# A two-block transformer kernel on one core: the normalising passes of five layer norms on VectorE instead of GpSimd, and half of a depthwise convolution as diagonal matmuls on TensorE

## What is computed

```python
h = layer_norm(ALPHA * h + 0.5 * swiglu_ffn(h, w13, w2), g0, b0)
h = layer_norm(ALPHA * h + token_mix(h, ...), g1, b1)
h = layer_norm(ALPHA * h + 0.5 * swiglu_ffn(h, w13, w2), g2, b2)
```

```python
u = a * sigmoid(gate)                 # a, gate: 256 columns each of h @ w_in
y = depthwise_conv(u, w_dw) + b_dw    # 31 taps, each channel for itself, left-padded
y = silu(layer_norm(y)) @ w_pw
```

## Time and profile before

| what | us |
|---|---|
| median of 3 runs | 1914.4 (1910.63 to 1915.46) |
| the profiled execution, its own time | 1913.0 |
| its span, first to last instruction | 1911.2 |
| TensorE busy | 1737.0 (91%) |
| VectorE busy | 1191.8 (62%) |
| ScalarE busy | 837.8 (44%) |
| GpSimd busy | 435.3 (23%) |
| mean granted TensorE clock | 0.956 of full speed |

### The profile page before, as it was taken

One profiled execution on the slowest core, in us unless ns is written; L12 is line 12 of the kernel. 1 busy time (PEld: TensorE's weight loads), 2 busy tenths in 40 slices (PEclk: granted clock), 3 DMA queues, 4 the chain that ended last, 5 costly groups with the idle time before them and its releaser, 6 DMA issues.

```text
span 1911.2 us, 32538 instructions
## 1 busy us (share of the span) xinstructions
PE 1737.0 (91%) x13186; PEld 1664.5 (87%) x13186; DVE 1191.8 (62%) x1561; ACT 837.8 (44%) x1116; POOL 435.3 (23%) x380
## 2 busy tenths in 40 slices
PE   7999968899999999968889996998999977779998
PEld 6999966699999999966689995987899976579997
DVE  5555588785556655587785544566656456466654
ACT  5334464353335333464353333663443346544333
POOL 0003576340045002576240042220000001300000
PEclk9999988999999999989999997997999989789999
DMA  6555433145543555423145542343355423025552
GB/s 214 172 174 201 150 103 105 66 144 180 179 181 131 176 176 191 156 103 110 67 167 176 192 182 88 114 141 111 111 182 209 172 96 116 17 103 192 180 204 82
DMA packets 37233, 277.67 MB, mean 145 GB/s; under 512 B 4304, under 2 KB 4432, under 8 KB 7072
## 3 DMA queue, kind: packets, MB, share of 16 engines
q1 hardware_dynamic: 36016, 271.73, 40.5%
q0 software_dynamic: 1136, 4.83, 0.7%
HBM read 275.49 MB, written 1.05 MB: 145 GB/s over the span
## 4 chain that ended last, share of the span: by engine, by line
PE 75%; DVE 12%; ACT 6%; POOL 3%; issue 3%; DMA 0%; SPq 0%; DVEq 0%; ACTq 0%; POOLq 0%
PE bank L635 23%; PE bank L637 23%; PE bank L636 23%; DVE w_lo L1679 3%; ACT w_hi L1156 2%; POOL y L566 2%; PE bank L653 1%; DVE conv_y L1958 1%; DVE rstd L1687 1%; DVE o_rstd L2047 1%; ACT h L1206 1%; ACT h_hi L1205 1%; POOL h L545 1%; ACT att_p L1482 0%; DVE qk_raw L1967 0%
## 5 line engine op out<-in xcount | busy, mean ns | idle before, releaser
L1679 DVE TENSOR_TENSOR w_lo<-raw,w_hi 128x2048 fp32r<-128x2048 f32 (+2 forms) x241 | 598.5, 2484 | 256.5 <-ACT w_hi L1156 256.0
L635 PE MATMUL bank<-h_hi,w_hi 128*128 128x272 f32 (+1 forms) x2336 | 676.3, 289 | 47.7 <-DVE w_lo L1679 27.0
L637 PE MATMUL bank<-h_hi,w_lo 128*128 128x272 f32 (+1 forms) x2336 | 674.2, 289 | 0.0
L636 PE MATMUL bank<-h_lo,w_hi 128*128 128x272 f32 (+1 forms) x2336 | 673.9, 288 | 0.0
L1156 ACT ACTIVATE w_hi<-raw 128x2048 fp32r<-128x2048 f32 (+2 forms) x241 | 486.1, 2017 | 144.6 <-PE bank L637 144.1
L635 PEld LDWEIGHTS bank<-h_hi,w_hi 128*128 128x128 f32 x2336 | 447.4, 192 | 52.0 <-DVE w_lo L1679 32.1
L637 PEld LDWEIGHTS bank<-h_hi,w_lo 128*128 128x128 f32 x2336 | 447.1, 191 | 0.0
L636 PEld LDWEIGHTS bank<-h_lo,w_hi 128*128 128x128 f32 x2336 | 446.5, 191 | 0.0
L635 PE MATMUL bank<-g_hi,w_hi 128*128 128x272 f32 (+1 forms) x1344 | 392.2, 292 | 12.5 <-DVE y L1705 4.9
L637 PE MATMUL bank<-g_hi,w_lo 128*128 128x272 f32 (+1 forms) x1344 | 386.2, 287 | 0.0
L636 PE MATMUL bank<-g_lo,w_hi 128*128 128x272 f32 (+1 forms) x1344 | 385.7, 287 | 0.0
(11 more groups left out here) (296 smaller groups left out, 1982.2 us busy)
## 6 DMA issues: line engine op xcount, KB each, us to landing
raw<-in_up_w SPq DMA_DIRECT2D x131, 1024.0 KB, 4.9
raw<-in_down_w SPq DMA_DIRECT2D x48, 1408.0 KB, 5.9
raw<-in_in_w SPq DMA_DIRECT2D x20, 1024.0 KB, 4.9
raw<-in_out_w SPq DMA_DIRECT2D x16, 1024.0 KB, 4.9
raw<-in_even_w SPq DMA_DIRECT2D x12, 1024.0 KB, 4.9
...
decay<-in_decay POOLq DMA_DIRECT2D x1, 1632.0 KB, 8.1
```

Source lines behind the costliest of these rows:

```text
L635: pe.matmul(out, w[0], x[0], start=first, stop=False)
L636: pe.matmul(out, w[0], x[1], start=False, stop=False)
L637: return pe.matmul(out, w[1], x[0], start=False, stop=last)
L1679: dve.tensor_tensor(w_lo[:, slot, 0:blocks * P], raw[:, slot, 0:blocks * P], w_hi[:, slot, 0:blocks * P].bitcast(F32), ALU.subtract).then_ ...
```

## The change

It has three parts.

1. The eight normalising passes of each norm are issued by VectorE (`renormalise`, in the order below) and no longer by GpSimd. The parts of VectorE's program around them are written in another order, and so are ScalarE's: the six later tiles stand in one row between the splits of chunks 3 and 4. A feed-forward block now defers three chunks, not four; chunk 3 goes to banks 6 and 7.
2. The 31 taps of channels 128 to 255 are matmuls: weights are 128x128 matrices with a tap's 128 coefficients on the diagonal, the moving operand is `upad` shifted by the tap, in plain float32, summed in bank 5. 16 taps stand in TensorE's program behind chunk 5 of the input product, 15 behind chunk 7. GpSimd's queue loads the matrices, 1 MB in front of each part, the second when the first is used. ScalarE copies the sum out with the bias, in chunk 9. The old product and addition loop on GpSimd is gone.
3. VectorE's half of the convolution adds even taps into `conv_y` and odd ones into `acc`, each waiting for the tap before the last, with one addition at the end.

The core of the diff. GpSimd:

```diff
-            def normalise():
...
-                for p in pairs:
-                    pool.tensor_tensor(p, p, both_tiles(mu), ALU.subtract).then_inc(t1_ready, 1)
-                pool.wait_ge(rstd_ready, seen.next(rstd_ready))
-                for p in pairs:
-                    pool.wait_ge(t1_ready, seen.next(t1_ready))
-                    pool.tensor_tensor(p, p, both_tiles(rstd), ALU.mult).then_inc(t_ready, 1)
...
                 pool.wait_ge(conv_in, seen.next(conv_in))
-
-                def product(i):
-                    if i >= 3:
-                        pool.wait_ge(conv_sum, seen.at(conv_sum, i - 1))
-                    pool.tensor_scalar(conv_t[:, i % 2, :], upad[:, 1, i:i + T], taps[:, i:i + 1], 0.0,
-                                       ALU.mult, ALU.add).then_inc(conv_mul, 1)
-
-                pool.tensor_scalar(conv_y[:, 1, :], upad[:, 1, 0:T], taps[:, 0:1], taps[:, TAPS:TAPS + 1],
-                                   ALU.mult, ALU.add).then_inc(conv_sum, 1)
-                product(1)
-                for i in range(1, TAPS):
-                    if i + 1 < TAPS:
-                        product(i + 1)
-                    pool.wait_ge(conv_mul, seen.at(conv_mul, i))
-                    pool.wait_ge(conv_sum, seen.at(conv_sum, i))
-                    pool.tensor_tensor(conv_y[:, 1, :], conv_y[:, 1, :], conv_t[:, i % 2, :], ALU.add)\
-                        .then_inc(conv_done if i == TAPS - 1 else conv_sum, 1)
-                seen.skip(conv_mul, TAPS - 1)
-                seen.skip(conv_sum, TAPS - 1)
+                pool.dma_start(diag[:], a["conv_w"][l, 0]).then_inc(diag_loaded, 16)
+                pool.wait_ge(diag_used, l + 1)
+                pool.dma_start(diag[:], a["conv_w"][l, 1]).then_inc(diag_loaded, 16)
                 residual_sums(2)
```

TensorE:

```diff
+                def conv_taps(c):
+                    for part in range(2):
+                        if c != CONV_AT[part]:
+                            continue
+                        pe.wait_ge(conv_in, l + 1)
+                        pe.wait_ge(diag_loaded, (2 * l + part + 1) * 16)
+                        for i in range(part * TAP_HALF, min((part + 1) * TAP_HALF, TAPS)):
+                            last = pe.matmul(ps[5][:, 0:T], diag[:, i % TAP_HALF, :], upad[:, 1, i:i + T],
+                                             start=i == 0, stop=i == TAPS - 1)
+                        last.then_inc(conv_mm if part else diag_used, 1)
+                in_tiles(IN_GROUPS, IN_ORDER, VALUES, [m for _, m in KTOK], 4, z_copied, T, conv_taps, DEFER)
```

ScalarE:

```diff
+            def renormalise(l, i):
+                split_next(UP_BLOCKS, 0, 2)
+                for k in range(2):
+                    normed_tile(l, i, k)
+                split_next(UP_BLOCKS, 0, 3)
+                for k in range(2, KD):
+                    normed_tile(l, i, k)
+                split_next(UP_BLOCKS, 0, 4)
...
+                            renormalise(*norm)
+                            deferred_silu(0)
+                            deferred_silu(1)
+                            split_next(UP_BLOCKS, 0, 5)
+                            deferred_silu(2)
...
+                def conv_copy(c):
+                    if c == 9:
+                        act.wait_ge(conv_mm, l + 1)
+                        act.activation(conv_y[:, 1, :], ps[5][:, 0:T], ACT.Identity, bias=vcol(l, V_CDB + 1))\
+                            .then_inc(conv_done, 1)
```

VectorE:

```diff
+            def renormalise(take):
+                pairs = [y[:, 2 * j:2 * j + 2, :] for j in range(KD // 2)]
+                def less_mean(j):
+                    dve.tensor_tensor(pairs[j], pairs[j], both_tiles(mu), ALU.subtract).then_inc(t1_ready, 1)
+                def by_deviation(j):
+                    dve.wait_ge(t1_ready, seen.next(t1_ready))
+                    dve.tensor_tensor(pairs[j], pairs[j], both_tiles(rstd), ALU.mult).then_inc(t_ready, 1)
 
                 dve.wait_ge(mean_ready, seen.next(mean_ready))
                 dve.tensor_scalar(mu[:], ps[6][:, 0:T], 1.0 / D, None, ALU.mult).then_inc(mu_ready, 1)
-                split_next(early, 0, 1)
+                split_next(UP_BLOCKS, 0, 1)
                 dve.wait_ge(var_ready, seen.next(var_ready))
                 dve.wait_ge(musq_ready, seen.next(musq_ready))
                 dve.scalar_tensor_tensor(musq[:], ps[7][:, 0:T], 1.0 / D, musq[:], ALU.mult, ALU.subtract)\
                     .then_inc(var_done, 1)
+                dve.wait_ge(mu_ready, seen.next(mu_ready))
+                less_mean(0)
+                less_mean(1)
                 dve.wait_ge(std_ready, seen.next(std_ready))
                 dve.reciprocal(rstd[:], std[:]).then_inc(rstd_ready, 1)
-                dve.wait_ge(mu_ready, seen.next(mu_ready))
                 dve.wait_ge(rstd_ready, seen.next(rstd_ready))
+                by_deviation(0)
+                split_next(UP_BLOCKS, 0, 2)
+                by_deviation(1)
+                less_mean(2)
+                less_mean(3)
+                by_deviation(2)
+                by_deviation(3)
+                split_next(UP_BLOCKS, 0, 3)
+                for k in range(4):
+                    low_tile(k)
+                take(0)
+                for k in range(4, KD):
+                    low_tile(k)
+                split_next(UP_BLOCKS, 0, 4)
+                take(1)
...
+                            renormalise(take)
+                            gated(0)
+                            split_next(UP_BLOCKS, 0, 5)
+                            take(2)
+                            gated(1)
+                            gated(2)
...
                 def conv_tap(i):
                     u, w = upad[:, 0, i:i + T], vcol(l, V_DW + i)
+                    out = acc[:] if i % 2 else conv_y[:, 0, :]
                     if i == 0:
-                        ins = dve.tensor_scalar(conv_y[:, 0, :], u, w, vcol(l, V_CDB), ALU.mult, ALU.add)
+                        ins = dve.tensor_scalar(out, u, w, vcol(l, V_CDB), ALU.mult, ALU.add)
+                    elif i == 1:
+                        ins = dve.tensor_scalar(out, u, w, None, ALU.mult)
                     else:
-                        ins = dve.scalar_tensor_tensor(conv_y[:, 0, :], u, w, conv_y[:, 0, :], ALU.mult, ALU.add)
+                        ins = dve.scalar_tensor_tensor(out, u, w, out, ALU.mult, ALU.add)
+                    ins.then_inc(dve_seq, 1)
+                    seen.skip(dve_seq, 1)
+                    dve.wait_ge(dve_seq, seen.at(dve_seq, 0 if i == TAPS - 1 else -1))
                     if i == TAPS - 1:
-                        ins.then_inc(conv_done, 1)
-                    else:
-                        link(ins)
+                        dve.tensor_tensor(conv_y[:, 0, :], conv_y[:, 0, :], acc[:], ALU.add).then_inc(conv_done, 1)
```

More of the change, by code:

```diff
@@ L42 @@
 TAPS = 31
+TAP_HALF = 16
 KTOK = [(0, 128), (128, 128), (256, 16)]
@@ L208, in forward @@
         conv_y = one("conv_y", [P, 2, T])
-        conv_t = one("conv_t", [P, 2, T])
-        taps = one("taps", [P, TAPS + 1])
         conv_sq = one("conv_sq", [P, 2, T])
```

131 lines of the change are left out of this document (39 added, 92 removed).

## The result

The changed kernel takes 1896.99 us (median of 4 runs, 1895.08 to 1901.92) against 1914.93 (4 runs, 1910.63 to 1916.65) of the kernel before on the same chip: ratio 0.9908, 95% interval 0.9891 to 0.9924. It is faster by 18 us, not by 4; I had forecast 1910.0 with a range from 1902. The profiled execution took 1896.89, its span is 1895.1, and the mean granted clock rose from 0.956 to 0.966.

A forecast was written before the change was run, and what follows sets the result against it. TensorE, busy 91% of the span, bounds the kernel, so only its waits can be won. Net 3.8 us at three norms and 0 at the input products, off 1913.0 or 1914.4, gave 1910.0, range 1902 to 1918.

The forecast's parts named there:

- The input products: Both layers' input products: 2.4 us lost, 1.9 and 1.1 saved, half a chance of losing 1.9; +0.3 each, taken as 0.
- Ahead of chunk 6: Input product: VectorE's stretch from chunk 5's `w_lo` falls from 17.7 to 13.1 us; chunk 6 starts at 271.5, not 276.6.
- Behind it: Input product after chunk 6 starts: 15 taps cost 7.5 us in full; the wait for the convolution's sum falls from 5.1 to some 4.
- The tap's price: Diagonal matmuls on TensorE in the input product: 0.5 us a tap at full clock, 8.0 for 16, 7.5 for 15.
- The rival of dear taps: TensorE's taps in the input products: at the half-clock price of 1.09 us each the kernel takes 1942; chance 0.09.
- that of late matrices: Loads of tap matrices for the input products: landing twice as late as the bound adds 13 us, 1922; chance 0.05.
- The norms: Three norms ahead of feed-forward blocks: gains 1.6, 1.8 and 4.2, less 1.5 and 2.3 for slow starts, net 3.8 us.
- The `w_lo` of 9.35: Third norm ahead of a feed-forward block: GpSimd's passes, not the table loads, stretch one `w_lo` from 2.29 to 9.35 us.
- The clock: Half-speed matmuls after TensorE's long waits: 1.9 us saved per input product, half a chance of losing it again; 2.3 deducted at norms.
- the gains come whole: Norms and input products: no slow starts after shorter waits, -7.6 and twice -0.6, so -8.8 us, 1905; chance 0.33.

The follow-up runs named there:

- norms_only: The kernel before with the change's norms alone: VectorE makes the passes, the convolution stays on GpSimd and VectorE; 1906.9 us, ratio 0.9960.
- ghost: The changed kernel with GpSimd also doing its old half of the convolution, into a tile nobody reads; 1914.8 us, ratio 1.0004.
- gp_taps_out: The kernel before without GpSimd's 30 further taps, so part of the output is not the reference's; 1899.6 us, ratio 0.9915.
- tables_away: The kernel before with the nine table loads moved from ahead of the last norm's passes to behind the sums that follow; 1911.7 us, ratio 0.9982.
- conv_only: The kernel before with the change's convolution alone, the passes staying on GpSimd; 1911.0 us, ratio 0.9978.

## Why the prediction was wrong

**The input products: the step that failed.** I wrote "+0.3, within the error of these prices; for two I take 0", and each gained 4.7. That is 9.4 of the 13 us that I was off. Most of the rest is the 2.7 us of the span outside the changed stretch. Against the +0.3 of the working the error is 5.0 a product, in two halves. *Ahead of chunk 6* (1.9): "the same order of passes brings VectorE to the end of chunk 5's `w_lo` at 255.8", 0.3 earlier than before, was 1.3 earlier, counted from the sums (1.0 of the error; in norms_only it is 1.1 earlier, so this is nearly all the passes' move). VectorE's stretch was 12.4 instead of 13.1. And my own terms, 255.8 + 13.1 + 2.3, make 271.2, where I wrote 271.5. That GpSimd's work beside it is what made the stretch 17.7 is shown by ghost and gp_taps_out; that mechanism I had right, only its size was short. *Behind it* (3.0, by 47.2 measured against 50.2): 15 taps cost 6.7 instead of 7.5; no slow start followed the wait of 1.0, where I had deducted half of one, 0.95; the wait for the convolution's sum fell to 3.4, not 4 (0.7, the two accumulators and the freed GpSimd); and a wait of 0.4 at a later chunk, which I hadn't counted, went. These are small terms, nearly all taken on the cautious side, and all in one direction.

**The tap's price.** 0.5 came from four instruction pairs over 2.10 us, and that stretch has the full duration of its last row, which is longer than the distance to a next one. From start to start (283.11 to 289.79 for 15) it is 0.445. The rival of dear taps had nothing in it: none of the 62 ran at half clock. Nor had that of late matrices: a load landed in 5.0 us, against the bound of 8.1.

**The norms: right in the sum, by errors that cancel.** Forecast 3.8 net. Sums to sums, the three gained 1.1, 1.4 and 1.4, 3.8. The chain was right: chunk 6 at +33.75, +33.73 and +34.59 against "+33.3 to +34", the wait at chunk 6 2.6 against 2.8 (33.3 less 30.4 and less the waits of 0.5 before it would have been 2.4), none over 0.25 at chunk 3, VectorE late next. The third fell short (2.9 to chunk 6, forecast 4.2 less 0.5) by the delayed transfer of chunk 3's weights, 0.9 ahead of chunk 4, which I had left out by saying that the loads stay. One slow start came (1.4); I had deducted 2.3. So the sum of 3.8 is met by luck.

**The `w_lo` of 9.35.** "I count it to the passes": with the passes gone it is 2.3, and the trace bears me out so far, but the alternative was drawn wrongly. Taking away the passes (norms_only, 2.3) or the loads (tables_away, 3.36) cures it. (The Trainium skill, SBUF — State Buffer, Who interferes with whom, adds that issue order decides who blocks. The rows fit it in tables_away: the `w_lo` that starts amid a pass stands still until that pass ends, and the next pass, 3.41 instead of 1.3 to 1.4, gives the time back. In the kernel before it starts amid a pass as well, and five more go ahead of it. What let them go first no run shows.)

**The clock.** I had it at next to nothing: 1.9 saved a product, half of that given back, and 2.3 deducted at the norms. It was 5.5 of the 13.4 us by the count above. Five of the eight slow starts in the stretch (7.2 us) had stood behind waits that the change removed or shortened; one of 1.4 came. Among the five is the one behind the 2.5 us at layer 1's chunk 3 (819.10), which my rows didn't have, since I read layer 0 and counted it twice. norms_only (2.0 less) and conv_only (0.8 more) show that most of it comes only with both parts.

**The rest.** Of the range, 1902 was the gains come whole and 3 more; the input product's own gain stood in none of the cases, so no case could reach 1897. What was missing is a rival in which GpSimd's contention frees more than the 15 exposed taps cost, with its prices at their low ends; the rows for it were there.
